# Forgetting attention: key biases subtracted on VectorE with the row maximum instead of added by matmuls

## The reference

```python
F = cumsum(log_sigmoid(f_pre), axis=1)          # per head and token
logits = einsum('bhqd,bhkd->bhqk', q_blk, k) * Dh ** -0.5 + (F_blk[..., :, None] - F[..., None, :])
logits = where(k_pos[None, :] <= q_pos[:, None], logits, -inf)
p = softmax(logits, axis=-1)
out = einsum('bhqk,bhkd->bhqd', p, v)
```

## Time and profile before

| | |
|---|---|
| median of 3 runs | 1978.67 us (1978.63 to 1978.91) |
| the profiled execution, first to last instruction (span) | 1976.6 us |
| median of the runs less this span | 2.1 us |
| TensorE busy | 1965.8 us, 99% of the span |
| VectorE, ScalarE, GpSimd busy | 856.3, 771.2, 610.4 us |
| attention stage | 1186 to 1404 us of the span |

### The profile page before, as it was taken

One profiled execution on the slowest core, in us unless ns is written; L12 is line 12 of the kernel. 1 busy time (PEld: TensorE's weight loads), 2 busy tenths in 40 slices (PEclk: granted clock), 3 DMA queues, 4 the chain that ended last, 5 costly groups with the idle time before them and its releaser, 6 DMA issues. The chain is left out here.

```text
span 1976.6 us, 27474 instructions
## 1 busy us (share of the span) xinstructions
PE 1965.8 (99%) x9500; PEld 1580.9 (80%) x9500; DVE 856.3 (43%) x1337; ACT 771.2 (39%) x1199; POOL 610.4 (31%) x241
## 2 busy tenths in 40 slices
PE   9999999999999999999999999999999999999999
PEld 6777878888888888888878877777788888888887
DVE  6888673332224443342284445555221363222200
ACT  7544442222223322232266566666422343322211
POOL 0000124444432344444313330000344423444443
PEclk9999999999999999999999999999999999999999
DMA  4111245543332555552212222112233323333322
GB/s 167 54 54 54 80 145 201 191 149 99 102 102 78 191 193 191 194 183 95 90 59 81 75 75 62 56 53 64 65 98 95 103 76 102 100 95 95 109 90 99
DMA packets 56644, 210.76 MB, mean 107 GB/s; under 512 B 6288, under 2 KB 7056, under 8 KB 56592
## 3 DMA queue, kind: packets, MB, share of 16 engines
q1 hardware_dynamic: 56592, 210.08, 33.1%
HBM read 207.96 MB, written 2.10 MB: 106 GB/s over the span
## 5 line engine op out<-in xcount | busy, mean ns | idle before, releaser
L382 POOL TENSOR_TENSOR wlo<-raw,whi 128x1024 fp32r<-128x1024 f32 (+1 forms) x234 | 603.0, 2577 | 1277.3 <-ACT whi L912 1277.3
L430 PE MATMUL bank<-xh,whi 128*128 128x512 f32 x1688 | 668.2, 396 | 3.8 <-DVE wlo L1452 1.3
L430 PE MATMUL bank<-xh,wlo 128*128 128x512 f32 x1688 | 657.9, 390 | 0.0
L430 PE MATMUL bank<-xl,whi 128*128 128x512 f32 x1688 | 657.4, 389 | 0.0
L912 ACT ACTIVATE whi<-raw 128x1024 fp32r<-128x1024 f32 (+1 forms) x298 | 330.6, 1109 | 618.2 <-PE bank L430 605.8
L430 PEld LDWEIGHTS bank<-xh,whi 128*128 128x128 f32 x1688 | 316.9, 188 | 84.7 <-issue 12.7
L430 PEld LDWEIGHTS bank<-xh,wlo 128*128 128x128 f32 x1688 | 316.8, 188 | 67.1
L430 PEld LDWEIGHTS bank<-xl,whi 128*128 128x128 f32 x1688 | 317.1, 188 | 64.2 <-issue 1.0
L430 PE MATMUL bank<-acth,whi 128*128 128x512 f32 x528 | 205.6, 389 | 0.2
L430 PE MATMUL bank<-actl,whi 128*128 128x512 f32 x528 | 205.4, 389 | 0.0
L430 PE MATMUL bank<-acth,wlo 128*128 128x512 f32 x528 | 205.4, 389 | 0.0
(11 more groups left out here) (322 smaller groups left out, 1914.5 us busy)
## 6 DMA issues: line engine op xcount, KB each, us to landing
raw<-w_dram SPq DMA_DIRECT2D x250, 512.0 KB, 3.6
adaw<-ada_dram SPq DMA_DIRECT2D x72, 512.0 KB, 4.3
raw<-wd_dram SPq DMA_DIRECT2D x48, 704.0 KB, 4.0
h<-x_dram SPq DMA_DIRECT2D x4, 512.0 KB, 7.0
out_dram<-h SPq DMA_DIRECT2D x8, 256.0 KB, 3.8
rel<-rel_dram SPq DMA_DIRECT2D x1, 513.0 KB, 6.5
crow<-c_dram SPq DMA_DIRECT2D x1, 512.0 KB, 3.6
gates_raw<-gates_dram SPq DMA_DIRECT2D x1, 384.0 KB, 4.5
```

Source lines behind the costliest of these rows:

```text
L382: nc.gpsimd.tensor_tensor(wlo[:, s, 0:width], raw[:, s, 0:width], whi[:, s, 0:width].bitcast(F32), ALU.subtract).then_inc(sem("w_lo"), 1)
L430: mm = nc.tensor.matmul(proj[b][:], w[:, s, W], v[:, k, :], start=first and j == 0 and a == 0, stop=last and j == len(chunks) - 1 and a == ...
```

## The change

The 64 bias products and their selector are dropped. SP stores the cumulated log decays (16 x 512) to a scratch tensor in DRAM during the mLSTM. For each pair of heads it loads the two rows back, broadcast to all 128 partitions (128 x 1024, 512 KB), into `fbias`, two such buffers laid over the work space of the norms. For the row maximum VectorE now uses one operation with two inputs: bank minus bias row, written to `fprob`, with the maximum of the result as its second output. ScalarE takes the exponential of `fprob` in place. TensorE's scores wait for the row maxima of the block before in place of its exponentials. VectorE's loop over six pairs is written out, the other engines' stay loops. In SP's program the slabs of this stage are loaded in loops of their own with the loads of the rows behind the first and the fourth slab of two pairs.

```diff
@@ -106,9 +106,12 @@
         ge = sb("ge", [P, P])
         geb = sb("geb", [P, P], BF16)
         leb = sb("leb", [P, P], BF16)
-        ssum = sb("ssum", [P, S])
-        sqn = sb("sqn", [P, 2, S])
-        rstd = sb("rstd", [P, S])
+        norms = sb("norms", [P, 4, S])
+        ssum, sqn, rstd = norms[:, 0, :], norms[:, 1:3, :], norms[:, 3, :]
+
+
+        fbias = norms[:].rearrange("p (a e) s -> p a e s", a=2)
+        fdram = nc.dram_tensor("fox_log_decays", (FH // 2, 2 * S), F32).ap()
         tmp = (sqn[:, 0, :], sqn[:, 1, :], ssum[:])
         gates_raw = sb("gates_raw", [P, KC * 96])
         stat = sb("stat", [P, 2, 8])
...
@@ -169,8 +172,6 @@
         yah = sb("yah", [P, KC, S], F32R, mix)
         yal = sb("yal", [P, KC, S], F32R, mix)
         sel = sb("sel", [96, MH, P], BF16, mix)
-        selp = sb("selp", [P, 2, P], F32R, mix)
-        fsp = sb("fsp", [P, S], F32R, mix)
         mls = ExitStack()
         ghi = sb("ghi", [P, KC * 96], F32R, mls)
         glo = sb("glo", [P, KC * 96], F32R, mls)
@@ -361,7 +362,31 @@
                         load_down(1, i, s - 1)
                     load_ada(i, 4 * ADA0 + 4 * (FC // 2 - 1), s)
             down_loop(1, first=1)
-            wide_loop(SLAB["mlstm"], (SLAB["down2"] - SLAB["mlstm"]) // 2)
+            wide_loop(SLAB["mlstm"], 4)
+            sp.wait_ge(sem("cum_f"), 1)
+            sp.dma_start(fdram.rearrange("t (e s) -> (t e) s", e=2), cs[32:32 + FH, :]).then_inc(sem("f_stored"), 16)
+            wide_loop(SLAB["mlstm"] + 8, (SLAB["fox"] - SLAB["mlstm"] - 8) // 2)
+
+            def load_decays(row, par, used):
+
+                sp.wait_ge(sem("rowmax"), used)
+                sp.dma_start(fbias[:, par].rearrange("p e s -> p (e s)"), fdram[row, :].to_broadcast([P, 2 * S])).then_inc(sem(f"f_in{par}"), 16)
+
+            sp.wait_ge(sem("f_stored"), 16)
+            load_decays(slice(0, 1), 0, AH * NB)
+            for s in range(6):
+                load_wide(None, 2, SLAB["fox"], s)
+            with sp.Fori(0, FH // 4 - 1) as i:
+                for s in range(6):
+                    load_wide(i, 6, SLAB["fox"] + 6, s)
+                    if s == 0:
+                        load_decays(bass.ds(i * 2 + 1, 1), 1, i * 16 + AH * NB)
+                    if s == 3:
+                        load_decays(bass.ds(i * 2 + 2, 1), 0, i * 16 + (AH * NB + 8))
+            load_wide(None, 2, SLAB["merge"], 0)
+            load_decays(slice(FH // 2 - 1, FH // 2), 1, (FH // 2 - 2) * 8 + AH * NB)
+            load_wide(None, 2, SLAB["merge"], 1)
+            wide_loop(SLAB["merge"] + 2, (SLAB["down2"] - SLAB["merge"] - 2) // 2)
             down_loop(2)
             base = TILE["down2"] // 2
             with sp.Fori(0, KC // 2) as i:
...
@@ -784,17 +809,12 @@
             def fox_scores(t, tt, b, beside=lambda: None):
 
                 W = (b + 1) * P
-                pe.wait_ge(sem("probs"), t * 8 + (UA + 2 * b))
+                pe.wait_ge(sem("rowmax"), t * 8 + (UA + 2 * b))
                 if b == 0:
                     pe.wait_ge(sem("f_qk"), primed(t * 2 + 2))
-                    pe.wait_ge(sem("f_sel"), t + 1)
                 for e in range(2):
                     H = slice(e * DH, e * DH + DH)
                     nc.tensor.matmul(bank[2 + e][:, 0:W], fq[H, tt, b * P:W], fk[H, tt, 0:W], start=True, stop=False,
-                                     skip_group_check=True)
-                for e in range(2):
-                    H = slice(e * DH, e * DH + DH)
-                    nc.tensor.matmul(bank[2 + e][:, 0:W], selp[H, tt, :], fsp[H, 0:W], start=False, stop=False,
                                      skip_group_check=True)
                 beside()
                 for e in range(2):
...
@@ -877,7 +897,6 @@
             wide("fox", 0, 6, 2, part=(7, KC))
             pe.wait_ge(sem("f_ln"), 1)
             wide("fox", 0, 6, 3, part=(0, 4))
-            pe.wait_ge(sem("f_rows"), 4)
             pe.wait_ge(sem("m_gated"), primed(MH * 2))
             fox_scores(0, 0, 0)
             wide("fox", 0, 6, 3, part=(4, KC))
@@ -1320,9 +1339,8 @@
             def fox_exps(t, k):
                 W = (k // 2 + 1) * P
                 act.wait_ge(sem("negmax"), t * 8 + (UA + k + 1))
-                act.wait_ge(sem("pT_ready"), t * 8 + (UA + k - 1))
                 st = stat[:, k % 2, :]
-                nc.scalar.activation(fprob[:, k % 2, 0:W], bank[2 + k % 2][:, 0:W], ACT.Exp, bias=st[:, 1:2],
+                nc.scalar.activation(fprob[:, k % 2, 0:W], fprob[:, k % 2, 0:W], ACT.Exp, bias=st[:, 1:2],
                                      accum_out=st[:, 2:3]).then_inc(sem("probs"), 1)
 
             def fox_copy(t, k):
@@ -1925,8 +1943,7 @@
             V.memset(qz[:, :, 0:CONV - 1], 0.0).then_inc(sem("pads"), 1)
             V.memset(zrow[:], 0.0).then_inc(sem("zeros"), 1)
             V.memset(mf[:], 0.0)
-            for t_ in (msM[:], fsp[:].bitcast(F32)):
-                V.memset(t_, 0.0).then_inc(sem("rows_clear"), 1)
+            V.memset(msM[:], 0.0).then_inc(sem("rows_clear"), 1)
             V.memset(mv[:, :, DV:DV + 1], 1.0).then_inc(sem("rows_clear"), 1)
             for g in range(MH):
                 V.tensor_scalar(sel[:, g, :], ones[0:96, :], c1("sel", g, rows=slice(0, 96)), None,
@@ -2036,12 +2053,6 @@
                                     ALU.subtract).then_inc(sem("m_y"), 1)
 
             convolve(0, 1)
-            fg = cs[32:48, :]
-            V.tensor_copy(fsp[32:48, :], fg).then_inc(sem("f_rows"), 1)
-            V.tensor_copy(fsp[96:112, :], fg).then_inc(sem("f_rows"), 1)
-            dve.wait_ge(sem("f_rows"), 1)
-            for at in (0, 64):
-                V.tensor_tensor(fsp[at:at + 16, :], fg, fsp[32:48, :].bitcast(F32), ALU.subtract).then_inc(sem("f_rows"), 1)
             with dve.Fori(0, MH - 1) as hd:
                 mlstm_head(hd)
             mlstm_head(MH - 1, more=False)
@@ -2049,8 +2060,17 @@
 
             UA = AH * NB
 
-            def fox_maxima(t, k):
-                maxima(t * 8 + UA, k, (k // 2 + 1) * P)
+            def fox_maxima(t, par, k):
+
+                e, W, st = k % 2, (k // 2 + 1) * P, stat[:, k % 2, :]
+                if k < 2:
+                    dve.wait_ge(sem(f"f_in{par}"), t * 8 + (16 - 8 * par))
+                dve.wait_ge(sem("scores"), t * 8 + (UA + k + 1))
+                dve.wait_ge(sem("probs_scaled"), primed(t * 8 + (UA + k - 1)))
+                V.tensor_tensor_reduce(fprob[:, e, 0:W], bank[2 + e][:, 0:W], fbias[:, par, e, 0:W], 1.0, -3.0e38, ALU.subtract, ALU.max,
+                                       accum_out=st[:, 0:1]).then_inc(sem("rowmax"), 1)
+                dve.wait_ge(sem("rowmax"), t * 8 + (UA + k + 1))
+                V.tensor_scalar(st[:, 1:2], st[:, 0:1], -1.0, None, ALU.mult).then_inc(sem("negmax"), 1)
 
             def fox_scale(t, k):
                 st = stat[:, k % 2, :]
@@ -2066,10 +2086,6 @@
                 dve.wait_ge(sem("f_rstd"), p * 2 + (2 - j))
                 V.scalar_tensor_tensor((fq, fk)[j][:, par, :], fraw[:, j, :], c1(("fox_q", "fox_k")[j], p), frs[:, j, :], ALU.mult,
                                        ALU.mult).then_inc(sem("f_qk"), 1)
-
-            def fox_selector(p, par):
-
-                V.tensor_scalar(selp[:, par, :], ones[:], c1("selp", p), None, ALU.mult).then_inc(sem("f_sel"), 1)
 
             def fox_pair(i, tt, more=True):
                 t = i * 2 + tt
@@ -2080,33 +2096,32 @@
                         fox_scale(t, 2 * b + 1)
                     if more and b == 2:
                         weight_low(i, 6, s, 2)
-                        fox_selector(t + 1, 1 - tt)
                     if b + 1 < NB:
-                        fox_maxima(t, 2 * b + 2)
-                        fox_maxima(t, 2 * b + 3)
+                        fox_maxima(t, tt, 2 * b + 2)
+                        fox_maxima(t, tt, 2 * b + 3)
                     if more and b == 0:
                         weight_low(i, 6, s, 1)
                 if more:
                     for j in (1, 0):
                         fox_normed(t + 1, 1 - tt, j)
                     weight_low(i, 6, s, 3)
-                    fox_maxima(t + 1, 0)
-                    fox_maxima(t + 1, 1)
+                    fox_maxima(t + 1, 1 - tt, 0)
+                    fox_maxima(t + 1, 1 - tt, 1)
                     fox_scale(t + 1, 0)
                     fox_scale(t + 1, 1)
                 dve.wait_ge(sem("yb_hi"), t + 1)
                 V.tensor_tensor(chunk(ybl, t), bank[7][:], chunk(ybh, t).bitcast(F32), ALU.subtract).then_inc(sem("yb_lo"), 1)
 
             dve.wait_ge(sem("q_scale"), 2)
-            fox_selector(0, 0)
+            dve.wait_ge(sem("f_stored"), 16)
             for j in (1, 0):
                 fox_normed(0, 0, j)
             for k in range(2):
-                fox_maxima(0, k)
+                fox_maxima(0, 0, k)
             weight_low(0, 6, SLAB["fox"], 4)
             for k in range(2):
                 fox_scale(0, k)
```

(12 more changed lines are left out.)

## The result

The changed kernel takes 1989.8 us (median of 4 runs, 1989.56 to 1990.16), the kernel before, on the same chip and in turn with it, 1978.8 (1978.63 to 1979.08). The ratio is 1.0056, with a 95% interval from 1.0044 to 1.0068: **slower by 11.0 us**, where 4.2 less was forecast. The span of the profiled execution went from 1976.6 to 1988.1 us, the granted clock is 1.00 in both.

A forecast was written before the change was run, and what follows sets the result against it. The prediction took TensorE's own stream to bound the attention stage; 4.3 us off for the bias products and 0.1 lost in the last pair took 1978.67 to 1974.5 us, with a range of 1973.4 to 1978.7.

The forecast's parts named there:

- Before the stage ... worth nothing: Ahead of attention, VectorE drops two copies and two subtractions, behind which it idled 1.99 us anyway: no gain.
- the sum: Whole kernel: 4.3 us gained, 0.1 lost, so 1978.67 - 4.2 = 1974.5 us, 0.21% less.
- waiting transposes: Rival, attention stage: new maximum slower still than the scan, TensorE's transposes wait, 16 us lost against 4.3, 1990; chance 0.05.
- late broadcasts: Rival, attention stage: bias-row broadcasts take past 28 us each, the maxima wait, 30 us more per pair, 2190; chance 0.03.
- The bias products: TensorE's stream in attention: removing 64 products saves 0.053 us per 128 columns, 0.53 per pair, 4.3 us in all.
- The rival in which the fixed part goes: Attention score groups: 32 times 0.11 us also saved, 3.5 more, 1971.0; chance 0.06, shared with the whole 17.73 going.
- The maxima: VectorE in attention: each of 64 new row maxima costs 0.08 us more, hidden behind TensorE's projection slabs.
- As slow as the scan: Rival, VectorE in attention: new maximum up to 0.60 us dearer at width 512, gain only 2.8, 1975.9; chance 0.11.
- The exponential: ScalarE in attention: reading SBUF instead of a bank, 644 ns against 691; off the path, worth nothing.
- The last pair: Last head pair of attention, with shorter slabs as cover: chain grows 0.16, shrinks 0.05, so 0.1 us lost.
- Waits and transfers: Attention stage: changed waits move nothing; eight 512 KB broadcasts land in 3.6 to 7.0 us and hide.
- it does not do what it says: Rival, attention stage: bias products ran in the drain of the scores, so nothing is gained, 1978.7; chance 0.04.

The follow-up runs named there:

- e9: The kernel before with its 64 bias products left out and all else, memory layout included, kept: 1973.95 us against 1978.48.
- e1: The changed kernel with an unused tensor of 32 bytes per partition that puts the later tensors back at their old alignment: 1974.09 us against 1978.61 for the kernel before.

## Why the prediction was wrong

**The step that failed** is "Before the stage ... worth nothing", and with it the sum, which took everything outside the attention stage as it was, a term of 0 us. Measured there are 15.3 us more on the 2352 products (8.1 ahead of the stage, 7.1 behind it). I went through the instructions that the diff removes and adds, and the addresses are none of them. The edit that cost 15.7 us is the shortest of the diff, a name less in the list of columns, and the prediction doesn't mention it. No row of before could price it: there all the products concerned lay at multiples of 256. What could have been seen is that it moves every later tensor, and that TensorE, busy for 99% of the span, spends most of it on such products of weights and activations. None of the rivals is this one; the slower rivals (waiting transposes, 1990; late broadcasts, 2190, which by its own terms should read some 2184) did not occur, and that the first of them names nearly the measured time is chance: the transposes waited 0.3 us.

**The bias products**: right in kind, 4.3 forecast, 4.7 measured. From a score group to the next group it takes 0.062 us less at width 128, 0.117 at 256, 0.174 at 384 and 0.234 at 512 (means of eight pairs), 0.59 for a pair and 4.7 for eight. That is in proportion to the width, 0.058 to 0.062 per 128 columns where I had 0.053, read from starts in steps of 0.01 us; the fixed 0.11 stayed, as forecast. The median of e9, 4.5 us less, agrees. The rival in which the fixed part goes (3.5 more) fell. Nor did 64 overheads of 60 cycles, which by the estimate from the page "TensorEngine Tiling (Array Packing)" of the Trainium skill would have added 1.6 us, come on top: with them it would be 5.9, measured are 4.5 to 4.7.

**The maxima**: right, 776 ns at width 512, hidden. "As slow as the scan" and "slower still" fell: the accumulator read is all that it costs over the plain reduction.

**The exponential**: wrong sign, no consequence. I took 47 ns less from a row of another function; it is 35 ns more at 512 columns (726 against 691), and 36 more at 128 (403 against 367).

**The last pair**: 0.1 us lost was forecast, with a wait near 0.4. In the timeline of the changed kernel TensorE waits 0.32 where it waited 0.26, so 0.06 are lost:

```profile
1405.91 0.42 PEld L829 LDWEIGHTS bank<-ident,fprob 128*128 128x128 f32 x4 [0.32 <-DVE fprob L2081]
```

**Waits and transfers**: right; 4.4 us to landing is inside 3.6 to 7.0, and no wait that names them appeared. "The broadcasts arrive late" fell, as did "it does not do what it says".

**The sum** without the addresses: e1 is the change as I had costed it, and gives 1974.09 where I said 1974.5. It was a forecast for that kernel, not for the one in the diff, and the 0.4 us between the two is the slope of the bias products read too low. For the changed kernel the first table adds up, from the traces alone, -4.7 on the scores, +15.3 on the 2352 products and +1.0 on all others: +11.6, where the medians differ by 11.0.

## What to carry to other kernels

A diff has a second effect beside its instructions: what it allocates, drops or resizes moves everything behind it, and on a kernel bound by TensorE that can outweigh the edit (here 15.7 us against 4.5). List the addresses of both versions, and compare groups of products that the diff does not touch; if their mean time moved, put the bytes back with a pad before judging the change. For fast float32 products like these, let the starts of weights and streamed operand lie a multiple of 256 bytes apart: no other distance tried here did as well.

## What the runs showed of the hardware

The fast float32 product of a 128 x 128 weight tile with 512 columns starts every 227 ns when the two operands' starts in SBUF differ by a multiple of 256 bytes, and 2 to 11 ns later for each of the other distances tried (4, 16, 32, 64, 96, 128, 224 bytes: 11.4, 5.2, 6.8, 2.1, 6.5, 6.0, 6.7). Moving both together by 32 or 128 bytes changes nothing, and the delay is the same whether ScalarE, VectorE and GpSimd work or not. I had not expected any such cost. The section Operand start alignment of the Trainium skill ("SBUF — State Buffer") asks an operand only to start at a multiple of its element size, and says that its runs timed nothing; every address here meets that rule, so the two do not contradict each other.

Why the distance counts is open. Each product here comes with a load of its own weights while the columns of the one ahead still stream (in the changed kernel the load from 529.98 to 530.17 us beside the product that starts at 529.97), so two reads of the same memory run at once, and one could delay the other by their relative place. That no other engine is needed fits this; no run here shows it. The odd order of the costs is not explained either, nor was it tried whether any distance does better than a multiple of 256, whether the products in plain float32 (the scores, whose operands both lie behind the table and kept their distance) or bf16 behave alike, or what fewer columns would do.
